# Products of constants in six pauses of TensorE, in a two-part transformer kernel on one core

## The reference, cut to what matters

```python
def rms_norm(x, g):
    xf = x.astype(F32)
    y = xf * lax.rsqrt(jnp.mean(xf * xf, axis=-1, keepdims=True) + EPS)
    return (y * g.astype(F32)).astype(x.dtype)

def first_block(...):
    ...
        merged = (g_a * branch_a.astype(F32) + g_b * branch_b.astype(F32)).astype(x.dtype)
        x = x + rms_norm(merged @ w_mix_out[l], norm_mix_post[l])
        h = rms_norm(x, norm_x_pre[l])
        mem_n = rms_norm(mem, norm_mem[l])
        x = x + rms_norm(memory_cross_attention(h, mem_n, w_xq[l], w_xkv[l], w_xo[l]), norm_x_post[l])
        h = rms_norm(x, norm_ff_pre[l])
        f = jnp.square(jax.nn.relu(h @ w_ff1[l])) @ w_ff2[l]
        x = x + rms_norm(f, norm_ff_post[l])
    return x

def hybrid_layer(x, norm_g, w_in, ...):
    h = rmsnorm(x, norm_g)
    proj = h @ w_in
    ...
    return x + acc @ w_out

def second_block(x, norm_g, w_in, ...):
    for l in range(DEPTH_2):
        x = hybrid_layer(x, norm_g[l], w_in[l], ...)
    return rmsnorm(x, final_norm_g)
```

## Time and profile before

| | |
|---|---|
| median of 3 runs | 2285.9 us (2285.89 to 2286.31) |
| the profiled execution's own time | 2281.14 us |
| its span in the trace | 2279.5 us |
| TensorE busy | 2162.6 us, 95% of the span |
| mean granted clock | 0.975 |
| next engines by busy time | VectorE 49%, ScalarE 44%, GpSimd 35% |

### The profile page before, as it was taken

One profiled execution on the slowest core, in us unless ns is written; L12 is line 12 of the kernel. 1 busy time (PEld: TensorE's weight loads), 2 busy tenths in 40 slices (PEclk: granted clock), 3 DMA queues, 4 the chain that ended last, 5 costly groups with the idle time before them and its releaser, 6 DMA issues.

```text
span 2279.5 us, 31042 instructions
## 1 busy us (share of the span) xinstructions
PE 2162.6 (95%) x11196; PEld 1775.5 (78%) x11196; DVE 1123.0 (49%) x2003; ACT 1005.2 (44%) x1950; POOL 792.6 (35%) x347
## 2 busy tenths in 40 slices
PE   5999999799989989999998999999999999999997
PEld 4788888678887878888886877878777777777776
DVE  5789999452542356452436523222286623222374
ACT  5767777652343442222223333434633433444631
POOL 2511111334464134444442423232343432232342
PEclk9999999899999999999998999999999999999998
DMA  4211111233233122232322222222223222222221
GB/s 145 84 61 65 64 60 60 74 120 102 93 126 96 38 83 74 94 100 93 102 92 88 93 65 75 68 72 71 87 84 125 83 84 64 67 69 71 76 94 63
DMA packets 51732, 189.32 MB, mean 83 GB/s; under 512 B 6564, under 2 KB 7204, under 8 KB 51108
## 3 DMA queue, kind: packets, MB, share of 16 engines
q1 hardware_dynamic: 48096, 175.13, 23.8%
q10 hardware_dynamic: 2452, 6.88, 0.8%
q0 software_dynamic: 1072, 5.77, 0.7%
HBM read 185.66 MB, written 2.10 MB: 82 GB/s over the span
## 4 chain that ended last, share of the span: by engine, by line
PE 77%; DVE 10%; ACT 5%; issue 3%; DVEq 3%; POOL 2%; DMA 0%; ACTq 0%; POOLq 0%
PE bank L350 21%; PE bank L352 20%; PE bank L351 20%; PE bank L933 2%; PE bank L976 2%; POOL weight_lo L382 1%; PE bank L959 1%; ACT weight_hi L376 1%; DVE wide_region L2225 1%; ACT wide_region L1059 1%; DVE wide_region L2228 1%; PE bank L425 1%; DVE h_lo L399 1%; PE bank L604 1%; PE bank L637 1%
## 5 line engine op out<-in xcount | busy, mean ns | idle before, releaser
L382 POOL TENSOR_TENSOR weight_lo<-weight_slots,weight_hi 128x1024 fp32r<-128x1024 f32 x277 | 674.6, 2436 | 1045.5 <-ACT weight_hi L376 1039.9
L376 ACT ACTIVATE weight_hi<-weight_slots 128x1024 fp32r<-128x1024 f32 x272 | 288.0, 1059 | 806.0 <-PE bank L352 720.3
L350 PE MATMUL bank<-h_hi,weight_hi 128*128 128x512 f32 x1144 | 464.5, 406 | 4.3 <-issue 3.0
L351 PE MATMUL bank<-h_lo,weight_hi 128*128 128x512 f32 x1144 | 449.6, 393 | 0.0
L352 PE MATMUL bank<-h_hi,weight_lo 128*128 128x512 f32 x1136 | 446.5, 393 | 0.0
L350 PEld LDWEIGHTS bank<-h_hi,weight_hi 128*128 128x128 f32 x1144 | 217.2, 190 | 52.4 <-issue 4.7
L352 PEld LDWEIGHTS bank<-h_hi,weight_lo 128*128 128x128 f32 x1136 | 215.4, 190 | 46.6
L351 PEld LDWEIGHTS bank<-h_lo,weight_hi 128*128 128x128 f32 x1144 | 217.6, 190 | 40.9
L382 POOL TENSOR_TENSOR head_weight_lo<-weight_slots,head_weight_hi 128x1024 fp32r<-128x1024 f32 x28 | 67.1, 2399 | 282.7 <-DVE v_region L1703 133.1
L350 PE MATMUL bank<-h_hi,head_weight_hi 128*128 128x512 f32 x336 | 139.8, 416 | 5.9 <-DVE h_lo L399 3.4
L352 PE MATMUL bank<-h_hi,head_weight_lo 128*128 128x512 f32 x336 | 132.9, 396 | 0.0
(11 more groups left out here) (489 smaller groups left out, 4468.4 us busy)
## 6 DMA issues: line engine op xcount, KB each, us to landing
weight_slots<-weights SPq DMA_DIRECT2D x328, 512.0 KB, 3.4
wide_region<-cmp_w ACTq DMA_DIRECT2D x2, 2048.0 KB, 9.3
v_region<-ssm_bc POOLq DMA_DIRECT2D x8, 256.0 KB, 4.5
residual<-x_in POOLq DMA_DIRECT2D x1, 2048.0 KB, 8.7
out<-normed SPq DMA_DIRECT2D x4, 512.0 KB, 2.7
residual<-x_in SPq DMA_DIRECT2D x2, 512.0 KB, 5.2
residual<-x_in ACTq DMA_DIRECT2D x2, 512.0 KB, 9.7
v_region<-mem_in POOLq DMA_DIRECT2D x1, 1024.0 KB, 5.2
```

The source lines that it names most:

```text
L350: pe.matmul(to, w_h[:, k, :], hi[:, k, 0:width], start=(k == 0), stop=False)
L351: pe.matmul(to, w_h[:, k, :], lo[:, k, 0:width], start=False, stop=False)
L376: act.activation(parts[0][s % 2], slot[s], ACT.Copy).then_inc(w_hi[s], 1)
L382: eng.tensor_tensor(parts[1][at], slot[s], parts[0][at].bitcast(F32), ALU.subtract).then_inc(w_lo[s], 1)
```

## The change

TensorE gets a helper that multiplies `IDENT_S` with the first 512 columns of `MASKS` into bank 5, n times, each product overwriting the one before. Nobody reads the result. The products wait for nothing and signal nothing. It is called in seven places, 85 products in all: 12 ahead of the first head's scores, 12 between sums and spread of norm 4 and 18 behind that spread, 8 and 18 at norm 6, 9 in layer L = 1 ahead of the first block on `H_HI`, 8 between sums and spread of norm 9. A wait for `masks_ready` is added once; the kernel before has the same wait a few instructions earlier. Other engines' programs are as they were.

```diff
+        def idle_products(pe, n):
+
+            for _ in range(n):
+                pe.matmul(bank[5][:, :], IDENT_S, MASKS[:, 0:T], start=True, stop=True)
@@ ahead of the heads
             pe.wait_ge(u_ready, KT)
+            pe.wait_ge(masks_ready, 1)
             s5_turn(0)
+            idle_products(pe, 12)
             da_score(0, 0)
             heads(pe, head_body)
@@ norm 4
             norm_sums(pe, 4, 5)
+            idle_products(pe, 12)
             norm_spread(pe, 4)
+            idle_products(pe, 18)
@@ norm 6
             norm_sums(pe, 6, 6)
+            idle_products(pe, 8)
             norm_spread(pe, 6)
+            idle_products(pe, 18)
@@ second part, layer L, behind scaled_terms(3, k)
+                if L:
+                    idle_products(pe, 9)
                 pe.wait_ge(evac_done[0], q0 + 1)
                 gemm(pe, q0 + 1, 0, H_HI, H_LO, T, SL * L + (S_L2 + S_H), own_bank=True)
```

## The result

The changed kernel takes 2265.15 us, median of 4 executions (2263.05 to 2267.12), against 2286.08 (2285.89 to 2286.31): ratio 0.9908, 95% interval 0.9891 to 0.9925. The forecast was 2267, within 2256 to 2279. The profiled execution took 2264.04 us, its span is 2261.6.

What follows compares the result with a forecast made beforehand. The prediction took TensorE's list of work to bound the kernel. From the profiled execution's 2281.1 us, touched places gave -11.8 (-2.0 - 2.3 - 4.8 - 2.7 + 0) and untouched ones -3: 2266; it predicted 2267, range 2256 to 2279.

Steps and rivals of the forecast that it cites:

- What bounds: Whole kernel: it is as long as TensorE's list takes, busy 95% of the span; only its pauses or pace give time.
- First head: Ahead of the first scores: twelve products overrun by 1.0 us, clock back at 108, stretch behind 3.05 shorter; net -2.0 us.
- Norm 4: Products fit both pauses; spread at full clock -1.0 us, first group of terms and sums behind it -1.3; sum -2.3.
- Norm 6: Clock already down, eight slow products overrun 1.4 us; spread's end moves +0.4, three groups behind gain 5.2; net -4.8.
- First block of layer 1: Nine products fit the 3.02 us pause; 13.5 matmuls behind take 3.1 instead of 5.8 us: -2.7.
- Norm 9: Eight products in a 2.02 us pause: gain 1.0 us or loss 1.4; taken as 0.
- Elsewhere: Untouched pauses: the change shifts later work, so clock falls there may go or come; -3 us, plus or minus 6.
- The offset of 4.8 us: Median of runs above the profiled execution, about three falls' cost; if of that kind, it need not recur; if constant, 2271.
- Rival 1: Products do not hold the clock, so those behind a fall run slow: about +10 us, 2296; chance 0.07.
- Rival 2: Local gains come, but five falls appear at pauses now harmless (+8 us) and none goes: 2282, no change; chance 0.09.
- Rival 3: Only the first head fails: products end at 110.3, overrun 2.4 us, gain 0.6 instead of 2.0: 2268; chance 0.1.
- Rival 4: Change does nothing since the pauses are bound elsewhere, by VectorE and GpSimd; only spread and paced terms gain; no own chance.

Runs made afterwards that it cites:

- run 2: Changed kernel with only the 8 and 18 products at norm 6 kept: 2269.33 us against 2277.47 for the kernel before, ratio 0.996.
- run 3: Kernel before plus eight products in a dense stretch near 65 us, none in a pause: 2280.3 us against 2277.47, ratio 1.0011.
- run 6: The kernel before once more, unchanged, for another profile: 2277.21 us, span 2275.5.
- run 7: Changed kernel with only the two rows of 18 behind the spreads of norms 4 and 6: 2269.28 us against 2282.81 before, ratio 0.9945.
- run 5: The changed kernel again, unaltered, with many executions: 2267.29 us against 2282.81 for the kernel before, ratio 0.9939.
- run 8: Changed kernel with further products in all pauses above 0.9 us where the clock ever fell: 2256.04 us against 2282.81 before, ratio 0.9889.
- run 1: Changed kernel with products of 32 columns instead of 512, in larger counts, in the seven places: 2289.24 us against 2277.47 before, ratio 1.0039.
- run 4: Changed kernel with all seven rows of products doubled: 2279.91 us against 2277.47 for the kernel before, ratio 0.9995.
- run 9: Kernel of run 8 with 6 products ahead of a deciding wait instead of 7 behind it: 2252.43 us against 2281.62 before, ratio 0.9875.

## Why the prediction was right

**What bounds.** Right: no other engine's busy time changed by more than 1 us, and nothing but TensorE's pauses and pace moved.

**First head,** forecast -2.0 (bounds -3.0 and +2.4), measured -2.9 in the first profile and -2.7 and -1.7 in the two others. The clock did not fall there in the first one, which is the bound without overrun; in the third it fell at 104.89 and the case was the one worked out. One step of that working was miscounted: with the clock back at 108 the row has 6.6 slow products and 5.4 fast ones and ends at 109.2, not 108.9, an overrun of 1.4 and a net of -1.7, which is what the third profile has. The mechanism was right, the likelier of its two cases was taken from a single profile. And the measure is a single profile too: in four others without a row there (runs 2, 3, 6, 7) the same place was 0.3 to 1.4 us shorter than in the first one.

**Norm 4,** forecast -2.3, measured -2.2, term by term: spread and what it releases -0.9, first group -1.4.

**Norm 6,** forecast -4.8, measured -6.2, with the clock never down, or -5.0 where it fell, just ahead of the row (run 2) or inside it (run 5). The step "here the clock had fallen before the eight products can begin" did not carry over from the kernel before: in all four profiles without a row ahead of this spread (before and runs 3, 6 and 7) the clock fell there ahead of the products' place, in the three of the changed kernel only once, and inside the row.

**First block of layer 1,** forecast -2.7, measured -2.7 in all three profiles of the changed kernel, against the first profile of before. Part of the match is luck: run 6 is the kernel before without any row and has no fall there, so it is 2.7 us shorter at this place too. Over the five profiles without a row there (before and runs 2, 3, 6 and 7) the fall cost 2.7, 1.6, 2.7, 0 and 1.6 us, so on average the row saves about 1.7. **Norm 9,** forecast 0, measured +0.1: the spread took 1.94 us, since the clock fell all the same, at 2250.39, inside the row of eight.

**Elsewhere,** forecast -3 plus or minus 6, measured -3.9, as the small rest of +5.5 and -9.7. Its price list had a slip: five stretches in all are of the kind that costs 1.6 us, not one and "five more"; the eighth is the 17 us at the memory norm, which got no price and was 2.4 us shorter than before when run 8 filled its pause. The reason given, that the change moves the later pauses, is only half of it. Run 6 shows that an unchanged kernel moves its falls by as much from one execution to the next, and the first comparison's 20.9 us contains about 5 of that. So that the time came out 2 us from the forecast is in part luck. With the averages above in place of single profiles, the touched places give about 11 us of the mean gain of 15.5 (an estimate from three profiles with the change and five without); as in run 7, the rest came at places left alone, and its cause stays open. Whether the shift as such has an effect on the mean could not be told: run 3, with a shift alone, came out 2.8 us above before for 1.8 us of added work, within its interval.

**The offset of 4.8 us** between the profiled execution and the median was held to be of the same kind. It is: 66 executions of before cover 2267 to 2287, and 2281.1 is an ordinary one.

**The rivals.** Rival 1 (the clock does not answer to such products) is wrong for products of 512 columns, in that they bring the clock back (run 7), and right for those of 32 (run 1). In part it holds for the wide ones too: the clock fell inside their rows at norm 9 and, in run 5, at norm 6. Rival 2 did not come; two falls appeared and two places cost more, as it said, but more went. Rival 3 did not come in the three profiles of the changed kernel; whether transposes count for the clock was not tried by itself, since the products cover them here. Rival 4 is settled by run 4: the pauses have no slack behind them.

## What to carry to other kernels

A pause of TensorE costs twice: its own length, and 1.6 to 6 us more where the clock falls in it (1.6 at 490, 6.2 at norm 6), which shows as the granted clock of the stretch behind it, not as idle time. Fill a pause with wide products of constants into a free bank, ahead of the wait that decides and a little shorter than the pause; a row too long is paid in full at 0.227 us a product, and a row behind the deciding wait too. Such a row does not always prevent the fall, but with one ahead of the spread and one behind it the stretch at 0.50 at norm 6 was 3.4 us (runs 2 and 5) in place of 20.5. Measure what a place costs in several profiles before counting on it. Before trusting a difference of under 1% in a kernel with many short pauses, time it often enough to see its spread, since a handful of executions can agree to 0.02% and still lie 6 us off the mean, as the first four of before did here (2285.9 to 2286.3 against 2280.3).

## What the runs showed of the hardware that was not expected

- TensorE can be busy without a gap, by the profile, and lose its clock: in run 1 it fell 2.3 us into a row of products of 32 columns, each with a full weight load, and stayed at 0.50 through 42 more of them, until 4.4 us of 512-wide terms had followed (17 us in all). The busy column does not tell what the clock will do; in the changed kernel the clock was at 1.00 over the 18 products of 512 columns in the same pause.
- The products multiply an identity by masks, so nearly all the terms that they add are zero, and this was no hindrance: in run 7 the clock came back within a row of them (at 837.36, the row from 833.00 to 839.41).
- Executions of one kernel on one chip differ by up to 20 us (2267.4 to 2287.3) through where the falls come; with the pauses filled they differ by 3 to 4 (runs 8 and 9, six each).
